# Where the gated sum of the last branch projection lives: its score bank in PSUM, or two buffers in SBUF

## The chip, the cores and the metric

One core of one Trainium2 chip. The metric is the device time of one execution in microseconds (us); less is better. The kernel before took 948.97 us (median of 3 runs, 947.03 to 949.14).

## The reference, cut to what matters

One layer of a streaming encoder, for 1024 prompt frames and 32 sample frames (T = 1056 tokens together), model width 1024, everything in fp32. Two attention branches A and B each give 512 features per token, and these are merged and projected out:

```
g_a, g_b = split(sigmoid(merge_logits))
mixed = g_a * (oa @ w_branch_a) + g_b * (ob @ w_branch_b)     # 512 -> 1024 features each
y = rmsnorm(x + mixed @ w_out) * norm_final_g                 # 1024 -> 1024 features
```

The kernel writes sigmoid(z) as 0.5 * (1 + tanh(z / 2)), and leaves the factor 0.5 to the output's last step.

## The kernel before, in words

Each fp32 product is made of three fp32r matmuls: every operand is split into a rounded part (hi) and the rest (lo), and hi·hi, hi·lo and lo·hi are added up in one PSUM bank (helper `three`, lines 1418 to 1422).

The engines run from one list of stages written out by `stage_list`; each engine walks the list and issues its part of each stage in order, with semaphores between them. Near the end of the list come 24 stages ("aunit", f, th), numbered v = 3f + th from 0 to 23. Unit v is feature tile f (128 features) times third th of the tokens (TH = 352) of `mixed`. Its parts:

- TensorE: 12 matmuls of `w_branch_a` with branch A's output into bank v % 4 of `score_banks` (`SC`). Unit v may overwrite its bank from unit v - 4 when `s_mixa` says that the first VectorE step of that unit is done (line 1495).
- VectorE, step 1 (line 1311, scalar_tensor_tensor): (1 + tanh gate A) * product, read from the bank, written to `mixw[v % 2]`, one of two SBUF buffers. It increments `s_mixa`. The gate is an SBUF tile (`feature_stage` or `tokens_stage` in the profile).
- VectorE, step 2 (line 1315, tensor_tensor): adds branch B's part `MB` (`mix_b` in the profile, SBUF) to `mixw[v % 2]` in place, and increments `s_mix`. The chain waits for step 1's own semaphore in between.
- ScalarE (line 974): rounds `mixw[v % 2]` into `MXH` (`mixed_hi`).
- VectorE, step 3 (`mixed_lo`, line 1105, tensor_tensor): `mixw` - `MXH` into `MXL` (`mixed_lo`). It is issued for unit v - 1 after step 2 of unit v. Step 1 of unit v waits until step 3 of unit v - 2 is done, as they share a buffer.

Between these units the list has "split" stages for the weights still to come: before units 0, 1, 3, 6, 8, 10, 11, 13, 15, 17 and 19 (`A_SPLITS`), for the weight tiles a1, o0, o1, a2, o2, o3, o4, a3, o5, o6, o7, where a is a pair of tiles of `w_branch_a` and o a tile of `w_out`. A weight comes by a DMA from SyncE into one of two `w_raw` buffers (lines 673, 678), ScalarE writes its hi part (line 623), GpSimd its lo part (`split_lo_late`, line 634). The load of the next weight is issued at the split before it, when GpSimd has freed the buffer. ScalarE does the split of a stage ahead of line 974 of that unit. Units 12 to 17 need a2, units 18 to 23 a3. SyncE also loads the gate tiles (line 764), in order of the list, each after a step 1.

Then TensorE makes the output product: for each of 9 token tiles and 2 halves e, product y = 2i + e, 24 matmuls of 512 columns (8 k steps of three) into bank y % 4. Products 0 to 3 wait for the bank's last unit by `s_mixa` (line 1682); step k also waits for the `MXL` it reads (`s_mxl`), which for product 0 and k = 7 is unit 21's. VectorE adds the residual (line 1406), and a norm and a store follow per tile.

Of the kernel before, what the change touches and what calls it, by code (L numbers as in the profile page):

```python
# [304 lines left out]
def hybrid_kernel(nc, a, o):  # L305
# [50 lines left out]
    with ctx:  # L356
# [89 lines left out]
        LW9 = g["LW"][:, :].rearrange("p (i f) -> p i f", i=NTT)  # L446
        def final_products(al):
            got = al("mixed_lo", [P, KD_, T], R), al("w_out_hi0", [P, KD_, 512], R)
            mix0 = al("mix_work0", [P, TH])
            al("da_branch_pad", [P, G_KEPT - H * T - KD_ * T - KD_ * 512 - TH])  # L450
            got += (al("da_branch_hi", [P, H, T], R), al("w_out_lo0", [P, KD_, 512], R))
            al("gate_place", [P, 2 * P + P + 64 + NTT * P + T + KC + (NTT + 2) * DV - KD_ * 512])
            return got + ([mix0, al("mix_work1", [P, TH])],)

        MXL, WOH0, BHA, WOL0, mixw = region(final_products)
        WOH, WOL = (WOH0, WOH1), (WOL0, WOL1)
        MXS = BHA[:, :, :].rearrange("p h t -> p (h t)")[:, 0:KD_ * 2 * DEC].rearrange("p (k b t) -> p k b t", k=KD_, b=2)

# [344 lines left out]
        def _(act):  # L803
# [8 lines left out]
            for st in stages:  # L812
# [133 lines left out]
                elif kind == "gK":  # L946
                    k, n = NTT * st[1] + st[2], ntok(st[2])
                    filled(act, st)
                    if k >= 2:
                        filled(act, ("gS",) + divmod(k - 2, NTT))  # L950
                    nc.scalar.activation(g["KDT"][k % 2][0:n, :], turn[0:n, 0:P], ACT.Copy).then_inc(free, 1)
                elif kind == "gO":
                    n = ntok(st[2])
                    filled(act, st)
                    if st[1] or st[2]:
                        act.wait_ge(s_gss, 2 * (NTT * st[1] + st[2]))
                    for e in range(2):
                        nc.scalar.activation(g["KSQ"][0:n, e, :], turn[0:n, GDV * e:GDV * (e + 1)], ACT.Square,
                                             accum_out=stat[0:n, 42 + e:43 + e]).then_inc(s_gss, 1)
                elif kind == "bsplit":  # L960
                    cols = slice(TH * st[1], TH * (st[1] + 1))
                    act.wait_ge(s_unit, unit_no(NP_ - 1, st[1]) + 1)
                    act.wait_ge(s_obld, 16)
                    nc.scalar.activation(BHB[:, :, cols], t_["OBS"][:, :, cols], ACT.Copy).then_inc(s_bh, 1)
                elif kind == "asplit":
                    h, t0, t1, upto = pieces[st[1]]
                    act.wait_ge(s_bl, 3)
                    freed(act, ("aO", h, upto - 1))
                    nc.scalar.activation(BHA[:, h, t0:t1], OAB[:, h, t0:t1], ACT.Copy).then_inc(s_ah, 1)
                elif kind == "aunit":  # L970
                    f, th = st[1], st[2]
                    v = 3 * f + th
                    act.wait_ge(s_mix, v + 1)
                    nc.scalar.activation(MXH[:, f, TH * th:TH * (th + 1)], mixw[v % 2][:, :], ACT.Copy).then_inc(s_mxh, 1)
                elif kind == "cache":
                    h = st[1]
                    filled(act, st)
                    nc.scalar.activation(t_["K"][h % 2][:, T:KC], turn[:, 0:PAST], ACT.Copy).then_inc(free, 1)
                elif kind == "aS":
                    h, i = st[1], st[2]  # L980
                    s = NTT * h + i
                    n, nk = ntok(i), cols_of(i)[1]
                    if s:
                        act.wait_ge(s_a, s)
                    else:
                        freed(act, ("gT", 1, NTT - 1))
                    if s >= 2:
                        h2, i2 = divmod(s - 2, NTT)
                        for q in range(len(groups(len(key_tiles(i2))))):
                            filled(act, ("aX", h2, i2, q))  # L990
                    for m in range(2):
                        act.wait_ge(s_nb, 2 * s + m + 1)
                        pm = t_["P0"][s % 2] if m == 0 else t_["P1"]
                        nc.scalar.activation(pm[0:n, 0:nk],  # L994
                                             SC[0:n, 2 * m:2 * m + 2, :].rearrange("p b c -> p (b c)")[:, 0:nk],
                                             ACT.Exp, bias=sm[0:n, s % 4, 2 + m:3 + m], scale=SCALE,
                                             accum_out=sm[0:n, s % 4, 4 + m:5 + m]).then_inc(s_ex, 1)
                elif kind == "aX":
                    h, i, q = st[1], st[2], st[3]
                    s = NTT * h + i  # L1000
                    n = ntok(i)
                    if s >= 2:
                        h2, i2 = divmod(s - 2, NTT)
                        filled(act, ("aV", h2, i2))
                    gr = groups(len(key_tiles(i)))[q]
                    filled(act, st)
                    for r, lo, hi in evac_parts(i, gr):
                        last = nc.scalar.activation(t_["AT"][s % 2][0:r, lo:hi, 0:n],  # L1008
                                                    psum3(turn, 4, P)[0:r, lo - gr[0]:hi - gr[0], 0:n], ACT.Copy)
                    last.then_inc(free, 1)  # L1010
                elif kind == "aQ":
                    h, i = st[1], st[2]
                    n = ntok(i)
                    act.wait_ge(s_oc, NTT * h + i + 1)
                    nc.scalar.activation(t_["OC"][0:n, :], t_["OC"][0:n, :], ACT.Square,
                                         accum_out=stat[0:n, 58:59]).then_inc(s_oss, 1)
# [57 lines left out]
        def _(dve):  # L1074
# [26 lines left out]
            def mixed_lo(v):  # L1101
                f, th = divmod(v, 3)
                cols = slice(TH * th, TH * (th + 1))
                dve.wait_ge(s_mxh, v + 1)
                nc.vector.tensor_tensor(MXL[:, f, cols], mixw[v % 2][:, :], MXH[:, f, cols].bitcast(F),
                                        ALU.subtract).then_inc(s_mxl, 1)

            for st in stages:
# [192 lines left out]
                elif kind == "aunit":  # L1301
# [3 lines left out]
                    dve.wait_ge(s_aunit, v + 1)  # L1305
                    if v == 0:
                        dve.wait_ge(s_tmst, 32 * 2 * H)
                    if v >= 2:
                        dve.wait_ge(s_mxl, v - 1)
                    dve.wait_ge(s_tld[(KD_ + f) % 3], 16 * ((KD_ + f) // 3 + 1))  # L1310
                    nc.vector.scalar_tensor_tensor(out=mixw[v % 2][:, :], in0=gates[(KD_ + f) % 3][:, cols], scalar=1.0,
                                                   in1=SC[:, v % 4, 0:TH], op0=ALU.add, op1=ALU.mult).then_inc(s_mixa, 1)
                    dve.wait_ge(s_mixa, v + 1)
                    dve.wait_ge(s_bout, u_last)
                    nc.vector.tensor_tensor(mixw[v % 2][:, :], mixw[v % 2][:, :], MB[:, f, cols], ALU.add).then_inc(s_mix, 1)
                    if v:
                        mixed_lo(v - 1)
                elif kind == "aN":
# [98 lines left out]
        def _(pe):  # L1417
# [6 lines left out]
            for st in stages:  # L1424
# [61 lines left out]
                elif kind == "aunit":  # L1486
# [5 lines left out]
                    if v < 4:  # L1492
                        pe.wait_ge(s_ex, 2 * H * NTT)
                    else:
                        pe.wait_ge(s_mixa, v - 3)
                    for k in range(H):
                        if v < 3:

# [178 lines left out]
            for i in range(NTT):  # L1677
                n = ntok(i)
                for e in range(2):
                    y = 2 * i + e  # L1680
                    if y >= 4:
                        pe.wait_ge(s_y2, y - 3)
                    else:
                        pe.wait_ge(s_mixa, 3 * KD_ - 3 + y)
                    if i == 0:
                        pe.wait_ge(s_wlo, NP_ + LATE.index(("o", 4 * e + 3)) + 1)
                    if i == TT:
                        pe.wait_ge(s_mxs, 2)
                    for k in range(KD_):
                        pe.wait_ge(s_mxl, 3 * k + 1 + min((P * i + n - 1) // TH, 2))  # L1690
                        if i == TT:
                            both = MXS[:, k, :, :].rearrange("p b t -> p (b t)")
                            out = SC[0:2 * n, y % 4, :]
                            nc.tensor.matmul(out, both, WOH[e][:, k, :], start=k == 0, stop=False)
                            last = nc.tensor.matmul(out, both, WOL[e][:, k, :], start=False, stop=k == KD_ - 1)
                            continue
                        last = three(SC[0:n, y % 4, :], MXH[:, k, tok(i)], MXL[:, k, tok(i)],
                                     WOH[e][:, k, :], WOL[e][:, k, :], k == 0, k == KD_ - 1)
                    last.then_inc(s_y, 1)
# [42 lines left out]
```

## Time and profile before

| | us |
|---|---|
| median of 3 runs | 948.97 |
| lowest, highest | 947.03, 949.14 |
| profiled execution, its own time | 948.3 |
| span of the profile (first to last instruction) | 946.5 |
| TensorE (PE) busy | 910.5, 96% |
| VectorE (DVE) busy | 485.8, 51% |
| ScalarE (ACT) busy | 364.3, 38% |
| GpSimd (POOL) busy | 122.6, 13% |

Busy shares are means over the whole span. PEld is TensorE's loading of stationary weights, which runs beside its matmuls. Matmuls are pipelined: one is recorded as longer than the distance to the next, so the distance between starts tells the rate. "idle before, releaser" is how long the engine had nothing to do before an instruction, and whose end let it go.

### The profile page before, as it was taken

The page shows a single profiled execution, that of the slowest core. Times are in us where ns is not written, and L with a number is a line of the kernel's source. Part 1 is how long each engine was busy: PE and PEld are TensorE (multiplying, and loading weights), DVE is VectorE, ACT ScalarE, POOL GpSimd, SP SyncE. Part 2 cuts the span into 40 slices and gives each one's busy share as a digit, 9 for nine tenths or more (in the row PEclk, how much of TensorE's full clock was granted, in tenths as well). Part 3 has the DMA queues.
Part 4 walks back from the last instruction along what each step waited for, and adds up shares of the span by engine and source line. Part 5 has one row for each costly group of instructions (what it writes and reads, how often), then busy time and mean ns, then how long its engine had stood idle before and what let it go on. Part 6 is the DMA issues. An engine that isn't in the chain of part 4 may idle for free. (4 is left out here: it accounts for less than half of the span.)

```text
span 946.5 us, 16619 instructions
## 1 busy us (share of the span) xinstructions
PE 910.5 (96%) x6648; PEld 831.3 (88%) x6648; DVE 485.8 (51%) x1098; ACT 364.3 (38%) x878; POOL 122.6 (13%) x210
## 2 busy tenths in 40 slices
PE   5899999999999999999999999999998999999997
PEld 4699999989999999999889899898997989988884
DVE  5623377741216776244643464455447676991223
ACT  6645354422335444134443353335334332430010
POOL 2001133210102222000000000000001103540000
PEclk9999999999999999999999999999999999999999
DMA  8022012213110213151032202121123325541222
GB/s 274 2 58 58 23 46 63 76 46 99 45 45 24 68 37 96 52 193 46 24 137 74 74 1 66 54 75 46 46 91 116 91 69 177 175 165 45 89 89 78
DMA packets 85903, 74.11 MB, mean 78 GB/s; under 512 B 4730, under 2 KB 78148, under 8 KB 85572
## 3 DMA queue, kind: packets, MB, share of 16 engines
q1 hardware_dynamic: 85828, 73.06, 25.4%
q8 instruction: 53, 0.87, 0.4%
q14 instruction: 22, 0.18, 0.1%
HBM read 53.32 MB, written 19.73 MB: 77 GB/s over the span
## 5 line engine op out<-in xcount | busy, mean ns | idle before, releaser
L1420 PE MATMUL proj_bank<-x_hi,w_hi 128*128 128x352 f32 x1056 | 350.9, 332 | 2.5 <-DVE w_lo L627 2.5
L1422 PE MATMUL proj_bank<-x_hi,w_lo 128*128 128x352 f32 x1056 | 340.2, 322 | 0.0
L1421 PE MATMUL proj_bank<-x_lo,w_hi 128*128 128x352 f32 x1056 | 339.6, 322 | 0.0
L1420 PEld LDWEIGHTS proj_bank<-x_hi,w_hi 128*128 128x128 f32 x1056 | 199.1, 189 | 4.8 <-DVE w_lo L627 2.8
L1421 PEld LDWEIGHTS proj_bank<-x_lo,w_hi 128*128 128x128 f32 x1056 | 199.6, 189 | 0.0
L1422 PEld LDWEIGHTS proj_bank<-x_hi,w_lo 128*128 128x128 f32 x1056 | 198.9, 188 | 0.0
L627 DVE TENSOR_TENSOR w_lo<-w_raw,w_hi 128x1024 fp32r<-128x1024 f32 x49 | 59.9, 1223 | 69.8 <-ACT w_hi L623 69.8
L994 ACT ACTIVATE probs<-score_banks,softmax_stats 128x128 f32<-128x128 f32 (+8 forms) x72 | 51.2, 713 | 78.1 <-DVE softmax_stats L1336 69.3
L1062 POOL TENSOR_TENSOR stats<-stats,minus_half 128x1 f32<-128x1 f32 (+1 forms) x36 | 22.4, 622 | 371.0 <-DVE stats L1369 371.0
L1047 POOL TENSOR_TENSOR decays<-log_decay 128x128 f32<-128x128 f32 (+1 forms) x122 | 47.6, 425 | 157.7 <-ACT log_decay L931 157.7
L623 ACT ACTIVATE w_hi<-w_raw 128x1024 fp32r<-128x1024 f32 (+1 forms) x53 | 55.1, 1039 | 17.2 <-PE proj_bank L1422 14.5
L872 ACT ACTIVATE feature_stage<-proj_bank 128x352 f32<-128x352 f32 x48 | 22.2, 461 | 95.6 <-PE proj_bank L1422 95.6
L1377 DVE SCALAR_TENSOR_TENSOR branch_out<-turn_bank,branch_norm_gains,da_gate 128x128 f32<-128x128 f32 (+1 forms) x36 | 12.2, 338 | 87.5 <-PE turn_bank L1674 87.5
L1333 DVE TENSOR_REDUCE softmax_stats<-score_banks 128x1 f32<-128x128 f32 (+8 forms) x72 | 51.4, 713 | 9.5 <-PE score_banks L1637 9.4
L1420 PE MATMUL score_banks<-w_out_hi,mixed_hi 128*128 128x512 f32 x128 | 50.6, 395 | 0.1
L1422 PE MATMUL score_banks<-w_out_hi,mixed_lo 128*128 128x512 f32 x128 | 50.4, 394 | 0.0
L1421 PE MATMUL score_banks<-w_out_lo,mixed_hi 128*128 128x512 f32 x128 | 50.3, 393 | 0.0
L1666 PE MATMUL turn_bank<-da_v,probsT 128*128 128x128 f32 (+2 forms) x312 | 44.2, 285 | 1.6 <-ACT probsT L1008 1.1
L1406 DVE SCALAR_TENSOR_TENSOR branch_out<-score_banks,branch_out 128x512 f32<-128x512 f32 (+1 forms) x18 | 12.4, 690 | 62.1 <-PE score_banks L1422 62.0
L1666 PEld LDWEIGHTS turn_bank<-da_v,probsT 128*128 128x128 f32 (+2 forms) x312 | 36.5, 185 | 6.9 <-issue 3.3
L1633 PE MATMUL score_banks<-da_k,da_q 64*128 64x512 f32 (+4 forms) x208 | 42.3, 509 | 0.0
L1026 ACT ACTIVATE feature_stage<-branch_out 128x1024 f32<-128x1024 f32 (+1 forms) x9 | 9.6, 1063 | 81.9 <-DVE branch_out L1406 81.9
(186 smaller groups left out, 1403.3 us busy)
## 6 DMA issues: line engine op xcount, KB each, us to landing
w_raw<-in_w_in SPq DMA_DIRECT2D x44, 512.0 KB, 4.6
merge_tanh_scratch<-feature_stage SPq DMA_DIRECT2D x16, 528.0 KB, 3.1
feature_stage<-merge_tanh_scratch SPq DMA_DIRECT2D x10, 528.0 KB, 3.6
x_rows<-in_x_prompt SPq DMA_DIRECT2D x8, 512.0 KB, 6.5
w_raw<-in_w_out SPq DMA_DIRECT2D x8, 512.0 KB, 4.5
branch_out<-in_x_prompt SPq DMA_DIRECT2D x8, 512.0 KB, 3.7
out<-branch_out SPq DMA_DIRECT2D x8, 512.0 KB, 2.6
tokens_stage<-merge_tanh_scratch SPq DMA_DIRECT2D x6, 528.0 KB, 3.7
```

Source lines behind the costliest of these rows:

```text
L623: nc.scalar.activation(halves(w)[0], raw[w % 2][:, :, 0:P if w else RANK], ACT.Copy).then_inc(s_whi, 1)
L627: nc.vector.tensor_tensor(halves(w)[1], raw[w % 2][:, :, 0:P if w else RANK], halves(w)[0].bitcast(F), ALU.subtract).then_inc(s_wlo, 1)
L872: nc.scalar.activation(FT[ft_no[t] % NFT][:, cols], bank, ACT.Tanh, scale=0.5).then_inc(s_uout, 1)
L994: nc.scalar.activation(pm[0:n, 0:nk], SC[0:n, 2 * m:2 * m + 2, :].rearrange("p b c -> p (b c)")[:, 0:nk], ACT.Exp, bias=sm[0:n, s % 4, 2 + ...
L1047: last = nc.gpsimd.tensor_tensor(g["E"][k % 2][:, l, 0:n].rearrange("p (b w) -> p b w", w=2 * w), b3, b3[:, :, w - 1:w].broadcast_to([P, n ...
L1062: nc.gpsimd.tensor_tensor(stat[0:n, 61:62], stat[0:n, 59:60], eps_pow[0:n, 0:1], ALU.pow).then_inc(s_ors, 1)
L1333: link(nc.vector.reduce_max(mm[:, m:m + 1], SC[0:n, 2 * m:2 * m + 2, :].rearrange("p b c -> p (b c)")[:, 0:nk], axis=AX.X))
L1420: nc.tensor.matmul(out, wh, xh, start=first, stop=False)
L1421: nc.tensor.matmul(out, wh, xl, start=False, stop=False)
L1422: return nc.tensor.matmul(out, wl, xh, start=False, stop=last)
L1633: done[m] = nc.tensor.matmul(SC[0:n, 2 * m + b, 0:w], t_["Q"][h % 2][r, tok(i)], t_["K"][h % 2][r, cc], start=True, stop=not masked)
L1666: last = nc.tensor.matmul(turn[0:n, 0:DV], t_["AT"][s % 2][0:w, e, 0:n], t_["V"][h % 2][0:w, vt, :], start=e == 0, stop=e == len(kt) - 1)
```

## The change

Steps 1 and 2 write into the unit's own score bank in place, ScalarE's rounding and step 3 read it there, and the two SBUF buffers go. Step 1's wait for step 3 of unit v - 2 goes too. Since the bank is now in use until step 3, TensorE's unit v waits for step 3 of unit v - 4 (`s_mxl`) where it waited for step 1 (`s_mixa`), and so do output products 0 to 3. One buffer's place in SBUF stays as padding, so nothing else moves.

```diff
-            mix0 = al("mix_work0", [P, TH])
+            al("mix_pad", [P, TH])
...
-            return got + ([mix0, al("mix_work1", [P, TH])],)
+            return got
...
 # ScalarE, aunit
                     act.wait_ge(s_mix, v + 1)
-                    nc.scalar.activation(MXH[:, f, TH * th:TH * (th + 1)], mixw[v % 2][:, :], ACT.Copy).then_inc(s_mxh, 1)
+                    nc.scalar.activation(MXH[:, f, TH * th:TH * (th + 1)], SC[:, v % 4, 0:TH], ACT.Copy).then_inc(s_mxh, 1)
...
 # VectorE, mixed_lo(v)
                 dve.wait_ge(s_mxh, v + 1)
-                nc.vector.tensor_tensor(MXL[:, f, cols], mixw[v % 2][:, :], MXH[:, f, cols].bitcast(F),
+                nc.vector.tensor_tensor(MXL[:, f, cols], SC[:, v % 4, 0:TH], MXH[:, f, cols].bitcast(F),
                                         ALU.subtract).then_inc(s_mxl, 1)
...
 # VectorE, aunit
-                    if v >= 2:
-                        dve.wait_ge(s_mxl, v - 1)
                     dve.wait_ge(s_tld[(KD_ + f) % 3], 16 * ((KD_ + f) // 3 + 1))
-                    nc.vector.scalar_tensor_tensor(out=mixw[v % 2][:, :], in0=gates[(KD_ + f) % 3][:, cols], scalar=1.0,
+                    nc.vector.scalar_tensor_tensor(out=SC[:, v % 4, 0:TH], in0=gates[(KD_ + f) % 3][:, cols], scalar=1.0,
                                                    in1=SC[:, v % 4, 0:TH], op0=ALU.add, op1=ALU.mult).then_inc(s_mixa, 1)
                     dve.wait_ge(s_mixa, v + 1)
                     dve.wait_ge(s_bout, u_last)
-                    nc.vector.tensor_tensor(mixw[v % 2][:, :], mixw[v % 2][:, :], MB[:, f, cols], ALU.add).then_inc(s_mix, 1)
+                    nc.vector.tensor_tensor(SC[:, v % 4, 0:TH], SC[:, v % 4, 0:TH], MB[:, f, cols], ALU.add).then_inc(s_mix, 1)
...
 # TensorE, aunit (v >= 4), and output products y < 4
-                        pe.wait_ge(s_mixa, v - 3)
+                        pe.wait_ge(s_mxl, v - 3)
...
-                        pe.wait_ge(s_mixa, 3 * KD_ - 3 + y)
+                        pe.wait_ge(s_mxl, 3 * KD_ - 3 + y)
```

## Rows read from the trace of the kernel before

**Rows 1.** The page: the span, and each engine's busy time, share and instructions.

```profile
span 946.5 us, 16619 instructions
PE 910.5 (96%) x6648; PEld 831.3 (88%) x6648; DVE 485.8 (51%) x1098; ACT 364.3 (38%) x878; POOL 122.6 (13%) x210
```

**Rows 2.** Windows: busy us (and instructions) of each engine, granted clock, DMA share.

```profile
792.20:842.50 50.30, 47.69 (x291) 46.43 (x290) 45.43 (x62) 20.53 (x31) 27.99 (x11) 1.00 0.57 170
842.50:931.70 89.20, 89.06 (x385) 71.86 (x385) 25.68 (x41) 10.49 (x19) 4.93 (x8) 1.00 0.25 90
```

**Rows 3.** Waits, 788 to 850 us: waiter <- releaser: us, times, longest.

```profile
PEld score_banks L1420 <- issue: 2.6, 4, 1.2
PE score_banks L1420 <- DVE mix_work L1311: 1.6, 3, 0.9
PE score_banks L1420 <- POOL w_lo L634: 1.0, 1, 1.0
PEld score_banks L1420 <- DVE mixed_lo L1105: 0.6, 1, 0.6
```

**Rows 4.** Timeline of TensorE: start us, duration us, instruction, idle before it.

```profile
792.22 0.32 PE L1420 MATMUL score_banks<-da_branch_hi,w_hi 128*128 128x352 f32 x1
...
805.81 0.32 PE L1420 MATMUL score_banks<-da_branch_hi,w_hi 128*128 128x352 f32 x1
...
829.57 0.43 PE L1420 MATMUL score_banks<-da_branch_hi,w_hi 128*128 128x352 f32 x1 [0.97 <-POOL w_lo L634]
...
842.49 0.39 PE L1420 MATMUL score_banks<-w_out_hi,mixed_hi 128*128 128x512 f32 x1
...
848.47 0.39 PE L1420 MATMUL score_banks<-w_out_hi,mixed_hi 128*128 128x512 f32 x1
```

**Rows 5.** Timeline of VectorE and GpSimd: two units, and step 3 of unit 20.

```profile
807.01 0.52 DVE L1311 SCALAR_TENSOR_TENSOR mix_work<-tokens_stage,score_banks 128x352 f32<-128x352 f32 x1
807.57 0.53 DVE L1315 TENSOR_TENSOR mix_work<-mix_work,mix_b 128x352 f32<-128x352 f32 x1
808.01 0.52 DVE L1105 TENSOR_TENSOR mixed_lo<-mix_work,mixed_hi 128x352 fp32r<-128x352 f32 x1
808.62 0.52 DVE L1311 SCALAR_TENSOR_TENSOR mix_work<-feature_stage,score_banks 128x352 f32<-128x352 f32 x1
...
836.11 0.52 DVE L1105 TENSOR_TENSOR mixed_lo<-mix_work,mixed_hi 128x352 fp32r<-128x352 f32 x1
836.14 2.75 POOL L634 TENSOR_TENSOR w_out_lo<-w_raw,w_out_hi 128x1024 fp32r<-128x1024 f32 x1 [1.94 <-ACT w_out_hi L623]
836.72 0.52 DVE L1311 SCALAR_TENSOR_TENSOR mix_work<-feature_stage,score_banks 128x352 f32<-128x352 f32 x1
837.27 2.00 DVE L1315 TENSOR_TENSOR mix_work<-mix_work,mix_b 128x352 f32<-128x352 f32 x1
...
845.48 0.52 DVE L1105 TENSOR_TENSOR mixed_lo<-mix_work,mixed_hi 128x352 fp32r<-128x352 f32 x1
```

**Rows 6.** By source line: durations min/median/max in ns, first and last start.

```profile
L1315 DVE TENSOR_TENSOR mix_work<-mix_work,mix_b x24: 524/526/1999, 794.9 to 848.3; 128x352 f32<-128x352 f32 x24
L1105 DVE TENSOR_TENSOR mixed_lo<-mix_work,mixed_hi x24: 510/518/2449, 797.3 to 849.4; 128x352 fp32r<-128x352 f32 x24
L1311 DVE SCALAR_TENSOR_TENSOR mix_work<-feature_stage,score_banks x15: 509/522/523, 794.4 to 841.4; 128x352 f32<-128x352 f32 x15
L1238 DVE TENSOR_TENSOR level_scores<-score_banks,level_masks x16: 681/692/693, 114.9 to 368.9; 128x512 f32<-128x512 f32 x16
```

**Rows 7.** A weight's way: its load, ScalarE's split, GpSimd's; then loads' landing times.

```profile
817.11 0.37 SPq L673 DMA_DIRECT2D w_raw<-in_w_out  x1
821.29 1.06 ACT L623 ACTIVATE w_out_hi<-w_raw 128x1024 fp32r<-128x1024 f32 x1 [1.68 <-DMA w_raw<-in_w_out]
822.43 2.42 POOL L634 TENSOR_TENSOR w_out_lo<-w_raw,w_out_hi 128x1024 fp32r<-128x1024 f32 x1 [0.66 <-ACT w_out_hi L623]
DMA to landing us min/median/max: 2.9/4.1/5.3
```

More of the change, by code:

```diff
@@ L452, in final_products @@
             al("gate_place", [P, 2 * P + P + 64 + NTT * P + T + KC + (NTT + 2) * DV - KD_ * 512])
-            return got + ([mix0, al("mix_work1", [P, TH])],)
-        MXL, WOH0, BHA, WOL0, mixw = region(final_products)
+            return got
+        MXL, WOH0, BHA, WOL0 = region(final_products)
         WOH, WOL = (WOH0, WOH1), (WOL0, WOL1)
```

## The prediction

> **What bounds the kernel now.** I read the page first: TensorE is busy 910.5 of 946.5 us [rows 1]. So only what moves TensorE counts, and the most that any change can win without taking matmuls away is its idle time. Next I asked for windows around the edited stage. In 792.20 to 842.50 TensorE is busy 47.69 us of 50.30, at full granted clock, and VectorE 45.43 us; in the output stage behind it TensorE is busy 89.06 of 89.20 [rows 2]. Nothing can be won behind the stage, only in it. The view of waits says what TensorE waits for there: step 1 of VectorE (1.6 us, 3 times), one lo part of a weight on GpSimd (1.0 us), unit 21's step 3 at output product 0 (0.6 us), and "issue" (2.6 us, the loads ahead of the same places, so not to be added) [rows 3].
>
> How much is that in all? I take it from starts, since matmuls overlap. Units 0 to 6 are 84 matmuls in 805.81 - 792.22 = 13.59 us: 0.1618 each, 1.94 us a unit. The output stage's are 89.20 us over 385, 0.232 each [rows 2]. Without a wait, product 1 would begin 288 x 0.1618 + 24 x 0.232 = 52.2 us after 792.22, at 844.4. It begins at 848.47 [rows 4]. **TensorE loses 4.1 us**, and this is the ceiling of the gain.
>
> Why does VectorE make it wait? Its timeline shows two kinds of unit. An undisturbed one, 807.01 to 808.62, costs 1.61 us, less than TensorE's 1.94. In a disturbed one step 2 takes 2.00 us, not 0.52: it starts at 837.27 while GpSimd works from 836.14 to 838.89, and ends 0.38 us after it [rows 5]. By line, the shortest step 2 is 524 ns and the longest 1999, and one step 3 took 2449 [rows 6]; in the timeline ten of the 24 step 2s are long. From unit 3 on it is nine, by 1.47 us each: 20 units from there take 20 x 1.61 + 9 x 1.47 = 45.4 us, 2.27 a unit against 1.94. **VectorE, held up by GpSimd, is the bound of this stage**, hidden by the four banks until about unit 16; then TensorE waits.
>
> **What is held up, and what isn't.** Step 1 at 836.72 lies wholly inside the same GpSimd instruction and takes 0.52 us [rows 5]; its longest is 523 ns [rows 6]. It has one input in SBUF and one in PSUM; steps 2 and 3 have two in SBUF. The other way round too: the GpSimd instruction that starts 0.03 us after a step 3 takes 2.75 us, one that starts free 2.42 [rows 5, 7]. So the two engines exclude each other where VectorE reads two SBUF tensors. After the change steps 2 and 3 read one from PSUM. The Trainium skill ("SBUF — State Buffer", section "Who interferes with whom") says the same as a rule: a VectorE instruction with at most one SBUF input, outside the two-port modes, doesn't contend with GpSimd. By it inputs decide, so an output in PSUM, which no row here has, would change nothing.
>
> **The change part by part.**
>
> *Steps 2 and 3 no longer held up.* Some 16 us leave VectorE: 9 x 1.47, 0.95 at unit 0, 1.93 of the one step 3. It is then at 1.61 us a unit, 0.33 under TensorE, and follows it from unit 0.
>
> *Price of the operands in PSUM.* Reading: a tensor_tensor of 512 columns from the bank and SBUF takes 692 ns, longest 693 [rows 6], so (512 columns against 352, at 0.17 us for 160) 0.52 at 352, as in SBUF. I take 0 for it. Writing to PSUM in place has no row. The nearest is step 1, which reads the same bank and writes to SBUF, 0.52 us: 0 extra is my value. From above, if a bank could only read or write in one cycle, steps 1 and 2 would pay 352 columns twice. By the slope of the two shapes that is 0.37 us more each, 0.89. From below: the shortest of all these forms is 509 ns [rows 6], so 0.01 each at the most. There is room: three steps can cost 1.94 - 0.05 (gaps net of overlap) together, 0.63 each, before VectorE bounds again. The Trainium skill ("VectorE: DVE Perf Modes", section on the TRN2 errata) charges a PSUM source 120 fixed cycles against 58 for SBUF, 65 ns more at 0.96 GHz; its "Rules for kernel authors" advise copying PSUM to SBUF first where many operations follow, which speaks against this change. The rows show no such difference, and with it added to two steps the unit would cost 1.74 us, still under 1.94: same sum.
>
> *ScalarE's rounding from PSUM*, 24 times 0.5 us: it has 30 us idle in the stage [rows 2]; nothing.
>
> *The removed wait* of step 1 for step 3 of v - 2: it is the instruction just ahead in VectorE's own queue, and the gap there is 0.09 us (808.01 + 0.52 to 808.62). At most 0.05 x 22 = 1.1 us of VectorE's time, hidden since TensorE is the bound.
>
> *The moved wait of TensorE.* Queued behind it are the next 12 matmuls and all that follow. Step 3 of v - 4 ends 1.52 us after step 1 of v - 3 starts (807.01 to 808.53), and that starts about 0.2 us after unit v - 2 does (unit 0's at 794.4 [rows 6], unit 1 at 794.16). Unit v starts two units, 3.88 us, after unit v - 2. Slack 3.88 - 1.73, less some 0.15 for the signal: 2.0 us. Product 0 waits for step 3 of unit 20: on the new clock that is ended by about 837 to 838.5, against a start at 838.8. No wait. Product 0's wait at k = 7 (0.6 us now) goes as well.
>
> *What is late next: the weights.* ScalarE splits a weight ahead of the unit's rounding, so a late load delays step 3, and by the new wait TensorE. The cycle of one buffer: load 4.2 us (817.11 to 821.29), split 1.06, GpSimd from 0.08 later for 2.42 [rows 7]: 7.75 us for every second weight. The splits from unit 11 on come every two units, so TensorE gives 4 x 1.94 = 7.76. Just even. But a load issued behind a gate tile takes longer; the loads spread from 2.9 to 5.3 us [rows 7]. Walk at 4.9 us: o2's load is issued behind the gate tile that waits for step 1 of unit 5 (over at 804.6), at 805.0, its lo is done 813.5; o4's at 822.0; o5's at 830.5; o7's raw at 835.4, its hi 836.5; rounding of unit 19 until 837.0, step 3 until 837.6; unit 23 could start at 836.8 and starts at 837.7, 0.9 us late. At 4.5 us each of the four loads is 0.4 earlier, and there is no wait. I take 0.3 us. The lo of a3, for which unit 18 now waits (829.57), is ready about 825, two us before unit 18 on the new clock (827.1): no wait.
>
> **Sum.** 948.3 (the profiled execution's own time, 1.8 above its span) - 4.1 + 0.3 = 944.5. The median of the runs is 0.7 above that execution; I put the median of after between 944.5 and 945.2: **944.8 us**. A difference under 0.3% (2.8 us) can't be told from none.
>
> **Rivals.**
> - *The weights take half of it back.* For: the cycle is even, and the four engines now push it earlier, into more overlap of loads. Against: ScalarE waits for a load only twice now. With loads at 5.3 us the same walk gives waits of 3.3 us; with 4.9 and some delay in steps, 1.7. Time 946.5.
> - *Only the waits on VectorE go.* The 1.0 of GpSimd's lo part and the "issue" may have another cause. Then 1.6 + 0.6 = 2.2 go: 946.1.
> - *In-place PSUM costs a second pass* (slower than before). At 0.89 us for steps 1 and 2 the unit costs 2.35 us, more than the 2.27 of now, and TensorE waits for step 3, not 1: step 3 of unit 20 ends at 794.4 + 21 x 2.35 + 2.25 - 0.61 (unit 0 has none behind it) = 845.4, and product 1 begins 0.15 + 5.6 later, at 851.1, not 848.5: 950.9. It decides from 0.69 us a step on (2 x 0.69 + 0.52 + 0.05 = 1.95). Against: nothing in the trace writes there; for: nothing either but the bank being shared.
> - *The hold-up stays* (slower; the change then doesn't free anything). If GpSimd held any VectorE instruction with an SBUF input and step 1 were the exception, the old pace stays. Step 3 of unit 20 ends at 846.0 (845.48 + 0.52 [rows 5]), product 0 starts there and not at 842.49, product 1 at 846.1 + 5.6 = 851.7: +3.2, 951.5. Against it: rows of steps 1 inside GpSimd's time, all 0.52.
>
> **Chances.** The forecast 0.62, weights 0.14, only VectorE's waits 0.10, second pass 0.08, hold-up stays 0.06. The forecast's own range is 943.6 to 946.2. The range for all, 943.0 to 948.0, leaves out the two slower cases and a little below. Faster by over 0.3% means under 946.1: nearly all of the forecast and a third of the two that stand at it, 0.66; slower 0.12; the rest 0.22.
>
> **What would show it.** Right: no step 2 or 3 over 0.6 us though GpSimd works beside it; GpSimd's splits all near 2.4; VectorE idle some 0.3 us each unit, released by TensorE; unit starts 1.94 us apart to the end; product 1 at 844.4 to 845.3. Wrong: steps 1 and 2 longer than 0.65; waits of TensorE on step 3; waits of ScalarE on the loads of o5 to o7 with TensorE waiting behind them.

## The result and the profile after

The changed kernel takes 943.32 us (median of 4 runs, 943.21 to 944.69), against 948.85 (4 runs, 947.03 to 949.14): a ratio of 0.9949, 95% interval 0.9932 to 0.9966. In five more runs beside nine of before it was 0.9950 (0.9937 to 0.9962), or 4.7 us (3.6 to 6.0). The profiled execution took 944.69 us against 948.3, so 3.6 less.

The page after: span, then each engine's busy time, share and instructions.

```profile
span 942.9 us, 16619 instructions
PE 909.6 (96%) x6648; PEld 832.2 (88%) x6648; DVE 470.0 (50%) x1098; ACT 362.9 (38%) x878; POOL 119.6 (13%) x210
```

VectorE is busy 15.8 us less than in [rows 1]. Here are the changed lines and GpSimd's, by source line: durations min/median/max in ns. Lines 1309 and 1313 are steps 1 and 2, which were 1311 and 1315.

```profile
L1309 DVE SCALAR_TENSOR_TENSOR score_banks<-feature_stage,score_banks x15: 519/529/530, 794.9 to 833.7; 128x352 f32<-128x352 f32 x15
L1313 DVE TENSOR_TENSOR score_banks<-score_banks,mix_b x24: 532/532/533, 795.4 to 840.1; 128x352 f32<-128x352 f32 x24
L1105 DVE TENSOR_TENSOR mixed_lo<-score_banks,mixed_hi x24: 514/515/525, 797.8 to 841.1; 128x352 fp32r<-128x352 f32 x24
L634 POOL TENSOR_TENSOR w_out_lo<-w_raw,w_out_hi x8: 2397/2408/2421, 800.1 to 834.9; 128x1024 fp32r<-128x1024 f32 x8
```

No step takes over 533 ns, where [rows 6] had 1999 and 2449. GpSimd's 2742 (median) are 2408. The timeline, VectorE and then GpSimd, shows that they do run beside each other: a step 3, a step 1, a step 2 and another step 3 all lie inside one GpSimd instruction, 827.28 to 829.69, of the kind that stretched the step 2 of [rows 5] to 2.00 us.

```profile
827.59 0.52 DVE L1105 TENSOR_TENSOR mixed_lo<-score_banks,mixed_hi 128x352 fp32r<-128x352 f32 x1 [0.58 <-ACT mixed_hi L974]
828.03 0.52 DVE L1309 SCALAR_TENSOR_TENSOR score_banks<-feature_stage,score_banks 128x352 f32<-128x352 f32 x1
828.58 0.53 DVE L1313 TENSOR_TENSOR score_banks<-score_banks,mix_b 128x352 f32<-128x352 f32 x1
829.02 0.52 DVE L1105 TENSOR_TENSOR mixed_lo<-score_banks,mixed_hi 128x352 fp32r<-128x352 f32 x1
...
827.28 2.41 POOL L634 TENSOR_TENSOR w_out_lo<-w_raw,w_out_hi 128x1024 fp32r<-128x1024 f32 x1 [2.47 <-ACT w_out_hi L623]
```

TensorE's starts, answering to [rows 4]: unit 0, output product 0, output product 1.

```profile
792.73 0.32 PE L1418 MATMUL score_banks<-da_branch_hi,w_hi 128*128 128x352 f32 x1
...
839.29 0.39 PE L1418 MATMUL score_banks<-w_out_hi,mixed_hi 128*128 128x512 f32 x1
...
844.86 0.40 PE L1418 MATMUL score_banks<-w_out_hi,mixed_hi 128*128 128x512 f32 x1
```

From unit 0 to product 1, **the stage**, it is 844.86 - 792.73 = 52.13 us against 848.47 - 792.22 = 56.25: 4.12 less. From product 1 to the end it is 98.04 against 98.03. Unit 0 began 0.51 later, which makes up the span's 3.6. In the window of the stage TensorE never stops (columns as in [rows 2]):

```profile
792.20:838.50 46.30, 46.30 (x289) 46.30 (x288) 33.65 (x68) 20.58 (x33) 26.43 (x11) 1.00 0.62 184
```

The waits of 788 to 850 us have no line of TensorE in the stage any more. Those of the others show what is late next, as these three:

```profile
ACT w_out_hi L623 <- DMA w_raw<-in_w_out: 12.0, 6, 2.9
DVE score_banks L1309 <- PE score_banks L1420: 9.0, 19, 1.4
DVE mixed_lo L1105 <- ACT mixed_hi L974: 2.5, 4, 1.0
```

VectorE now waits for TensorE at 19 of the 24 units, and ScalarE waits 12.0 us for tiles of `w_out` where it waited 3.1. Four times the lateness reaches step 3, never TensorE. The latest step 3 is that of unit 11: it ends at 820.76, and unit 15, which waits for it, begins at 821.83, 1.1 us later. An undisturbed one has 2.2 us (step 3 of unit 3 ends at 804.14, unit 7 begins at 806.32).

### The profile page after: what moved, and what is told of

Its sections match the earlier page's. It is cut to its first block, busy times and chain, and to the rows that moved or that the text cites. A ratio compares the mean times of both kernels' runs of the same rounds, so it can differ in the third digit from the quotient of the medians.

```text
span 942.9 us, 16619 instructions
## 1 busy us (share of the span) xinstructions
PE 909.6 (96%) x6648; PEld 832.2 (88%) x6648; DVE 470.0 (50%) x1098; ACT 362.9 (38%) x878; POOL 119.6 (13%) x210
## 4 chain that ended last, share of the span: by engine, by line
PE 92%; DVE 3%; ACT 2%; issue 2%; DMA 1%; POOL 0%; SPq 0%; DVEq 0%; POOLq 0%; ACTq 0%
PE proj_bank L1418 20%; PE proj_bank L1420 19%; PE proj_bank L1419 19%; PE score_banks L1418 5%; PE score_banks L1420 5%; PE score_banks L1419 5%; PE turn_bank L1664 4%; PE score_banks L1631 4%; PE turn_bank L1648 2%; PE turn_bank L1520 1%; PE turn_bank L1579 1%; PE score_banks L1564 1%; PE turn_bank L1582 1%; DVE branch_out L1280 1%; PE score_banks L1444 1%
```

## The experiments

"Stage" is from unit 0's first matmul to output product 1's, in each kernel's profiled execution. The ratio is to the kernel before, with its 95% interval.

| kernel | stage, us | ratio |
|---|---|---|
| before | 56.25 | |
| changed | 52.13 | 0.9949 (0.9932 to 0.9966) |
| 1 changed, again | 52.13 | 0.9950 (0.9937 to 0.9962) |
| 2 only TensorE's waits moved | 60.09 | 1.0038 (1.0026 to 1.0051) |
| 3 before, GpSimd writes zeros | 52.13 | 0.9950 (0.9937 to 0.9964) |
| 4 changed, step 1's wait kept | 52.13 | 0.9953 (0.9940 to 0.9965) |
| 5 step 2 writes to SBUF | 54.76 | 0.9981 (0.9972 to 0.9990) |
| 6 changed, GpSimd's lo parts twice | 61.68 | 1.0044 (1.0028 to 1.0060) |
| 7 before, zeros three times | 52.12 | 0.9941 (0.9924 to 0.9958) |
| 8 before, GpSimd copies | 52.13 | 0.9946 (0.9931 to 0.9960) |

**1. The changed kernel again.**

> The changed kernel once more, in more rounds. The trace accounts for 4.1 us (all of TensorE's waits in the stage). The medians so far differ by 5.5, with an interval of 3.2 to 6.5. If 4.1 is all, the difference over more rounds comes out at 3.6 to 4.8 us; if the change gives something more outside the stage, at 5 or over.

The medians (948.78 and 943.77) differ by 5.0 us, the ratio makes it 4.7 (3.6 to 6.0): this lies between the two expected ranges and decides nothing. The profiled execution does decide for the stage: 52.13 once more, with 98.0 us behind it. What is left is the part ahead of unit 0, which no edit touches and which differs among executions: unit 0 began between 790.8 and 792.7 in the ten profiled ones. Part of it is the granted clock. Windows of 40 to 60 us, first of the changed kernel, then of experiment 4:

```profile
40.00:60.00 20.00, 17.48 (x101) 16.61 (x100) 6.46 (x16) 7.00 (x14) 0.00 (x0) 0.91 0.20 54
```

```profile
40.00:60.00 20.00, 17.48 (x111) 16.67 (x109) 6.21 (x16) 7.01 (x14) 0.00 (x0) 1.00 0.20 54
```

At a mean clock of 0.91 TensorE got through 101 matmuls there, at 1.00 through 111. The kernel before met the 0.91 too in its profiled execution, so the pair of profiles compared above doesn't differ by it. There the clock was at 0.50, the lower of the two levels (1.2 GHz), from 48 to 50 us, after TensorE had been busy for only 0.04 us of the 2 us before that; experiment 4 had the same gap and stayed at 1.00. Unit 0 began at 791.9 to 792.7 in the three profiled executions with the 0.91, and at 790.8 to 791.3 in the seven without.

Every execution has its mean granted clock on record, and most of what the medians have over 4.1 goes with it. At 0.998 the kernel before took 946.81 to 948.10 us (4 executions) and the changed one 942.89 to 943.36 (5): their medians are 3.9 apart. At 0.997 (10 and 4 executions) they are 4.1 apart. But the kernel before was at 0.996 in 15 of 32 executions, the changed one in none of 9. Why it is there more often is open, and the clock isn't all: three executions of the kernel before at 0.999 took 947.95 to 949.29.

**2. Only TensorE's waits moved.**

```diff
 # the kernel before
-                        pe.wait_ge(s_mixa, v - 3)
+                        pe.wait_ge(s_mxl, v - 3)
...
-                        pe.wait_ge(s_mixa, 3 * KD_ - 3 + y)
+                        pe.wait_ge(s_mxl, 3 * KD_ - 3 + y)
```

> Buffers in SBUF as before, only TensorE's waits moved to step 3. Theory (VectorE's pace is set by GpSimd's hold-ups, and the changed kernel can afford the later wait only as these are gone): step 3 of unit 20 ends at 846.0, product 0 waits for it, product 1 begins near 851.7 and not 848.5: 3.2 us slower than before, 952. Rival (the waits on VectorE are small whatever step they are for): within 1 us of before.

Slower by 3.6 us (2.5 to 4.8); the stage is 3.84 longer, near the 3.2 expected. The waits, with the line of TensorE that [rows 3] had on step 1:

```profile
PE score_banks L1420 <- DVE mixed_lo L1105: 5.8, 9, 1.1
PEld score_banks L1420 <- issue: 5.2, 7, 0.8
```

TensorE waits for step 3 nine times. The last of these waits is unit 23's, for step 3 of unit 19, and output product 0 follows it without another:

```profile
843.84 0.40 PE L1420 MATMUL score_banks<-da_branch_hi,w_hi 128*128 128x352 f32 x1 [0.58 <-DVE mixed_lo L1105]
...
845.86 0.39 PE L1420 MATMUL score_banks<-w_out_hi,mixed_hi 128*128 128x512 f32 x1
```

The later wait is dear by itself, and free once nothing stretches VectorE's steps. Taken in this order, the two halves of the change are worth +3.8 (the wait) and -8.0 us (the operands in PSUM) in the stage.

**3. GpSimd writes zeros.**

```diff
 # the kernel before, split_lo_late
-            nc.gpsimd.tensor_tensor(halves(w)[1], raw[w % 2][:, :, :], halves(w)[0].bitcast(F),
-                                    ALU.subtract).then_inc(s_wlo, 1)
+            nc.gpsimd.memset(halves(w)[1].bitcast(F), 0.0).then_inc(s_wlo, 1)
```

> The kernel before, with GpSimd's 11 late lo parts of weights left out: it writes zeros in their place and reads nothing. Theory (step 2 and 3 are held up because GpSimd reads SBUF while they read two SBUF tensors): steps 2 and 3 all near 0.52 us, TensorE's 4.1 us of waits go, 944.8. Rival (any GpSimd instruction in SBUF holds them up): long steps 2 remain, each as long as the GpSimd instruction beside it lasts; time between the two.

The stage is 52.13 with the SBUF buffers in place. The longest step 2 and step 3 are 527 ns. One step 3 beside GpSimd:

```profile
829.40 0.53 DVE L1104 TENSOR_TENSOR mixed_lo<-mix_work,mixed_hi 128x352 fp32r<-128x352 f32 x1
...
829.04 0.95 POOL L634 MEMSET w_out_lo<- 128x1024 f32 x1 [3.57 <-ACT w_out_hi L623]
```

Taking GpSimd's reads away, with VectorE's steps, the buffers and the waits as before, gives the whole gain in the stage, so the gain there is the hold-up. But each pass of zeros is also short, 0.95 us; hence the next.

**7. Zeros three times over.** The memset of experiment 3 is issued three times for each weight, each after the one before it.

> The kernel before, with each of GpSimd's 11 late lo parts left out and zeros written in its place three times over, about 2.9 us, longer than the lo part's 2.4. Theory (only a GpSimd instruction that reads SBUF holds up steps 2 and 3): no step over 0.55 us, the stage as short as with one pass of zeros, 944. Rival (the single pass of zeros was only too short to do harm): holds of up to 0.95 us for each of the 33 passes, and TensorE's waits are partly back, 945 to 948.

GpSimd works 2.9 us for each weight, more than the 2.4 of the subtraction. Steps 2 and 3 still take 0.52 and 0.53, and the stage 52.12. The rival falls: it is the reading, not the length.

**8. GpSimd copies.**

```diff
 # the kernel before, split_lo_late
-            nc.gpsimd.tensor_tensor(halves(w)[1], raw[w % 2][:, :, :], halves(w)[0].bitcast(F),
-                                    ALU.subtract).then_inc(s_wlo, 1)
+            nc.gpsimd.tensor_copy(halves(w)[1], raw[w % 2][:, :, :]).then_inc(s_wlo, 1)
```

> The kernel before, with GpSimd's 11 late lo parts replaced by a copy of the raw weight (the subtraction is left out): one input read from SBUF, not two. Theory (reading at all is enough): steps 2 and 3 that start inside such a copy wait for its end, as now, only for the shorter time that a copy may take (some 1 to 2 us); stage between 52.1 and 56.3 us. Rival (it takes two inputs on GpSimd's side too): no step over 0.55 us, 52.1.

A copy has one input in SBUF, and this is enough. VectorE and then GpSimd:

```profile
811.35 1.23 DVE L1314 TENSOR_TENSOR mix_work<-mix_work,mix_b 128x352 f32<-128x352 f32 x1
...
814.10 0.52 DVE L1104 TENSOR_TENSOR mixed_lo<-mix_work,mixed_hi 128x352 fp32r<-128x352 f32 x1
...
811.16 1.04 POOL L634 CAST w_out_lo<-w_raw 128x1024 fp32r<-128x1024 f32 x1 [3.37 <-ACT w_out_hi L623]
814.12 1.40 POOL L634 CAST w_out_lo<-w_raw 128x1024 fp32r<-128x1024 f32 x1 [1.92 <-ACT w_out_hi L623]
```

Step 2 started inside the first copy (811.16 to 812.20) and took 1.23 us; the second copy started inside a step 3 and took 1.40, not 1.04. Whoever comes second waits for the end of the other's instruction. This is so each time: the ten stretched steps here end 0.37 to 0.38 us after the copy that they started in, and those of the kernel before 0.38 to 0.39 after the subtraction. Yet the stage is at 52.13: the ten holds are 0.1 to 0.8 us each and some 4.6 in all, less than the 24 x 0.33 = 7.9 us that VectorE has over in the stage. A hold-up is only worth something from the sum at which VectorE falls behind.

**4. Step 1's wait kept.**

```diff
 # the changed kernel
+                    if v >= 2:
+                        dve.wait_ge(s_mxl, v - 1)
                     dve.wait_ge(s_tld[(KD_ + f) % 3], 16 * ((KD_ + f) // 3 + 1))
```

> The changed kernel with step 1's wait for step 3 of unit v - 2 put back. Theory: it waits for what VectorE itself has just issued, at most 0.05 us a unit, under the 0.4 that VectorE idles per unit: same time as the changed kernel within 0.3 us. Rival (part of the gain is from dropping it): up to 1.1 us back.

The stage is the same 52.13, the ratio 0.9953 beside 0.9950 for the changed kernel against the same executions of before. The dropped wait is worth nothing.

**5. Step 2 writes to SBUF.**

```diff
 # the changed kernel, with the two SBUF buffers back
+                    if v >= 2:
+                        dve.wait_ge(s_mxl, v - 1)
-                    nc.vector.tensor_tensor(SC[:, v % 4, 0:TH], SC[:, v % 4, 0:TH], MB[:, f, cols], ALU.add).then_inc(s_mix, 1)
+                    nc.vector.tensor_tensor(mixw[v % 2][:, :], SC[:, v % 4, 0:TH], MB[:, f, cols], ALU.add).then_inc(s_mix, 1)
...
 # rounding and step 3 read mixw; TensorE, v >= 4 (and likewise y < 4)
-                        pe.wait_ge(s_mxl, v - 3)
+                        pe.wait_ge(s_mix, v - 3)
```

> Steps 1 and 2 work on the score bank, but step 2 writes to the two SBUF buffers, and rounding and step 3 read there; TensorE waits for step 2 of unit v - 4. Now only step 3 has two SBUF inputs. Theory (what counts is two SBUF inputs beside a reading GpSimd, whichever step): hold-ups move to step 3, some ten of 1.5 to 2 us, VectorE stays near 2.2 us a unit, and the time is within 1.5 us of before, 947.5 to 949. Rival (step 2 alone is the trouble, or its in-place form): no hold-ups, 944.8.

The timeline of VectorE and GpSimd shows the hold-up on its new place:

```profile
829.33 0.53 DVE L1315 TENSOR_TENSOR mix_work<-score_banks,mix_b 128x352 f32<-128x352 f32 x1
829.77 1.72 DVE L1105 TENSOR_TENSOR mixed_lo<-mix_work,mixed_hi 128x352 fp32r<-128x352 f32 x1
...
828.55 2.56 POOL L634 TENSOR_TENSOR w_out_lo<-w_raw,w_out_hi 128x1024 fp32r<-128x1024 f32 x1 [2.94 <-ACT w_out_hi L623]
```

Step 2, with one SBUF input, runs through inside GpSimd's instruction. Step 3, with two, is stretched: it ends at 831.49, 0.38 us after GpSimd's instruction, and this happens ten times in the stage. The mechanism came as expected; the time is 1.8 us (0.9 to 2.7) under before, 946.5, a little below the 947.5 to 949 expected. TensorE waits for step 2 here, which comes ahead of the stretched one.

**6. GpSimd's lo parts twice.**

```diff
 # the changed kernel, split_lo_late: ahead of the subtraction, the same once more
+            nc.gpsimd.tensor_tensor(halves(w)[1], raw[w % 2][:, :, :], halves(w)[0].bitcast(F),
+                                    ALU.subtract).then_inc(s_gp2, 1)
+            pool_.wait_ge(s_gp2, w - LATE_POOL + 1)
```

> The changed kernel with each of GpSimd's 11 late lo parts computed twice, 4.85 us in place of 2.4. Theory (the weights' cycle of load, split and lo part was just even with TensorE, so the changed kernel has little room there): the cycle is 10.2 us for two weights against 7.76, TensorE waits in units 12 to 21 for step 3 or for the lo part of a2 or a3, some 9 us in all: 953. VectorE's steps stay at 0.53. Rival (the weights have ample room): no change from the changed kernel, 944.8.

952.1 us, stage 61.68: 9.55 longer than the changed kernel's, where the walk along the weights gave 9 for the waits. The waits:

```profile
ACT w_out_hi L624 <- DMA w_raw<-in_w_out: 26.3, 8, 3.9
DVE mixed_lo L1109 <- ACT mixed_hi L978: 18.1, 10, 3.8
```

No hold-up comes with twice the GpSimd work: line 1317, step 2, stays at 532 ns. It is the cycle of load, split and lo part. This is the bound that stands next to TensorE in this stage.

Not all of the 9.55 us is waiting. After its longest idle time, 3.14 us up to 824.36, TensorE was granted the lower clock for about 3 us (columns as in [rows 2]):

```profile
825.00:828.00 3.00, 3.00 (x12) 3.00 (x12) 1.61 (x4) 1.22 (x2) 2.92 (x2) 0.50 0.92 276
```

Its matmuls start 0.293 us apart there (11 distances from 824.75 to 827.98), not 0.162. That is 1.5 us, so the waits themselves are 8.1 where 9 was expected. What the stage would have been at full clock isn't shown: a later wait, for the lo part of a3, may have taken the place of the 1.5.

## Why the prediction was right

- **The ceiling of 4.1 us** read from TensorE's starts was the gain in the stage, 4.12. Over whole executions it was 4.7 to 5.5, with intervals that hold 4.1, and 3.9 to 4.1 between executions of like clock (experiment 1).
- **The hold-up and its end**: steps 2 and 3 near 0.52, GpSimd's parts at 2.4, 15.8 us less of VectorE (some 16 foretold). Experiments 3, 7 and 8 show the cause from GpSimd's side, 5 from VectorE's.
- **Operands in PSUM**: 0 was taken for it; step 2 pays 6 ns, step 3 nothing. Step 1 takes 529 ns, 7 more than before, but written in place it took 518 to 521 (medians) in experiments 5 and 6, where it seldom had to wait for TensorE just before. A second pass over the bank (0.89 us a step) isn't there.
- **The removed wait**: nothing, as costed (experiment 4).
- **The moved wait**: hidden, as costed: 2.0 us of slack were foretold, 2.2 is what an undisturbed unit has and 1.1 the least. With the hold-ups kept it costs 3.84 in the stage where the rival "the hold-up stays" said 3.2 (experiment 2). The rival took the wait of product 0 for step 3 of unit 20 as the one that binds. That step ended at 845.31, but product 0 began at 845.86: what bound it was unit 23, let go by step 3 of unit 19 (over at 843.70) and 2.02 us long. This is 0.4 of the missing 0.6; the other 0.2 is VectorE, counted from unit 0, which was late by that from unit 12's step 2 on (2.19 us there, not 2.00).
- **The weights** were the term mis-sized: 0.3 us foretold, 0 measured. The walk took 4.9 us for each of four loads. In the changed kernel those of o2, o4, o5 and o7 landed in 4.9, 4.8, 3.8 and 4.0 us, so it was right for two of them and 2.0 too long in the other two. The splits were late all the same (12.0 us of ScalarE's waiting), but what of it reached step 3, at most 1.0 us, ended in the slack of the moved wait. That the cycle is near is shown by experiment 6.
- **The other waits**: the rival that only VectorE's own 2.2 us would go is refuted. TensorE's waits for GpSimd's a3 and on "issue" went as well. The lo part of a3 was done at 824.8 (825 foretold), when unit 18 was still 2.8 us away.

The forecast of 944.8 is 1.5 above the measured median, 943.32, which lies 0.3 below the forecast's own range (943.6 to 946.2) and inside the range for all cases (943.0 to 948.0). 0.3 of the 1.5 is the weights. The rest is ahead of the stage, where the profiled executions differ by up to 2 us: the prediction put the median up to 0.7 above the profiled execution, as with the kernel before (948.97 against 948.3), and it came out 1.4 below (943.32 against 944.69). That it stayed inside the wide range is in part luck; the stage is where the reasoning was tested.

## What to carry to other kernels

Where VectorE's instructions of one shape have two lengths in the trace, look for GpSimd beside the long ones, and count how many SBUF tensors each reads. An operand that is left in PSUM takes the instruction out of the conflict, even if its bank is then held longer; check first that the engine that wants the bank back still has slack once the long ones are gone. Before adding up what a faster engine brings, take the starts of the engine that bounds: ideal pitch times count against the real distance is the ceiling, and here it was the gain.

## What the runs showed of the hardware

- A VectorE instruction with two SBUF inputs and a GpSimd instruction with even one exclude each other, both ways round. A VectorE step of 0.52 us that comes second ends 0.37 to 0.39 us after GpSimd's (kernel before, experiments 2, 5 and 8); a GpSimd instruction that comes second, just after a step's start, takes 0.3 to 0.4 us longer. A GpSimd memset of 128x1024, 0.95 us, doesn't disturb (experiments 3 and 7), and a VectorE step with one SBUF input isn't disturbed (changed kernel, experiments 5 and 6).
- VectorE's fp32 addition of 128x352 takes 532 ns in place in a PSUM bank, 524 from that bank to SBUF (experiment 5) and 526 from SBUF to SBUF. Step 1's form (scalar_tensor_tensor), in place, takes 514 to 530 ns (changed kernel, experiments 4 to 6), the longer ones mostly right behind a wait for TensorE; to SBUF its median is 522. ScalarE's copy of that shape takes 463 ns from PSUM and 498 from SBUF.
- GpSimd's subtraction of 128x1024 takes 2.40 us undisturbed, its copy 1.04.
